# Retention two halves denser, outputs turned in the narrow chunk, and gates of the second half with silu at eviction

## What is computed

```
for l in range(DEPTH):                                  # 2 layers
    mod = silu(c) @ w_mod[l] + b_mod[l]                 # 2048 x 6144
    shift, scale, gate = split(mod, 3)
    h = rmsnorm(x, norm_gain[l]) * (1 + scale) + shift
    proj = h @ w_in[l]                                  # 2048 x 7504
    q_a, k_a, v_a, g_a, q_i, k_i, w_i, q_b, k_b, v_b, g_b = split(proj)
    y_a = sparse_attention(...) * silu(g_a)             # 8 heads of 128
    ret = retention(rotary(q_b), rotary(k_b) * SCALE, v_b)   # 8 heads of 128
    y_b = head_groupnorm(ret, ret_norm_gain[l]) * silu(g_b)
    x = x + gate * (concat(y_a, y_b) @ w_out[l])        # 2048 x 2048
```

## Time and profile before

| | us |
|---|---|
| median of 3 runs | 1963.54 |
| lowest, highest | 1959.96, 1964.26 |
| the profiled execution's own time | 1960.76 |
| span of its trace | 1959.0 |
| PE, DVE, ACT, POOL busy | 1877.9, 1363.6, 966.3, 326.2 |

### The profile page before, as it was taken

One profiled execution on the slowest core, in us unless ns is written; L12 is line 12 of the kernel. 1 busy time (PEld: TensorE's weight loads), 2 busy tenths in 40 slices (PEclk: granted clock), 3 DMA queues, 4 the chain that ended last, 5 costly groups with the idle time before them and its releaser, 6 DMA issues.

```text
span 1959.0 us, 24539 instructions
## 1 busy us (share of the span) xinstructions
PE 1877.9 (96%) x9056; PEld 1565.5 (80%) x9056; DVE 1363.6 (70%) x1953; ACT 966.3 (49%) x1307; POOL 326.2 (17%) x395
## 2 busy tenths in 40 slices
PE   4989999999888999999999999999999999999995
PEld 4878778888766877888878888888888888878884
DVE  8989989887788996755565544488775466564544
ACT  5454455444524444554454544566664445443643
POOL 0000002182203000217220000044440020030000
PEclk9999999999988999999999999999999999999998
DMA  9979967766585994654455555554445555556551
GB/s 351 355 247 345 348 226 275 280 221 212 197 309 184 340 356 163 195 168 155 144 178 188 189 193 193 194 172 151 150 152 179 193 184 180 189 182 213 184 174 65
DMA packets 210767, 420.08 MB, mean 214 GB/s; under 512 B 7136, under 2 KB 12012, under 8 KB 209772
## 3 DMA queue, kind: packets, MB, share of 16 engines
q1 hardware_dynamic: 209004, 413.08, 62.6%
q10 hardware_dynamic: 1664, 5.66, 0.8%
HBM read 416.59 MB, written 2.11 MB: 214 GB/s over the span
## 4 chain that ended last, share of the span: by engine, by line
PE 91%; DVE 6%; ACT 1%; issue 1%; POOL 0%; DMA 0%; DVEq 0%; ACTq 0%; POOLq 0%
PE acc L585 27%; PE acc L587 27%; PE acc L586 27%; DVE scr L1644 2%; PE tps L679 2%; DVE w_lo L1525 1%; PE sps L892 1%; PE sps L706 1%; PE tps L626 1%; PE tps L557 1%; PE acc L706 0%; PE tps L730 0%; PE sps L756 0%; DVE proj L1617 0%; PE sps L755 0%
## 5 line engine op out<-in xcount | busy, mean ns | idle before, releaser
L1525 DVE TENSOR_TENSOR w_lo<-raw,w_hi 128x1024 fp32r<-128x1024 f32 (+1 forms) x596 | 757.7, 1279 | 513.8 <-ACT w_hi L1069 501.4
L1069 ACT ACTIVATE w_hi<-raw 128x1024 fp32r<-128x1024 f32 (+1 forms) x596 | 623.5, 1051 | 801.4 <-PE acc L587 694.7
L585 PE MATMUL acc<-w_hi,ht_hi 128*128 128x512 f32 (+1 forms) x2384 | 946.4, 397 | 19.0 <-DVE proj L1888 9.0
L587 PE MATMUL acc<-w_hi,ht_lo 128*128 128x512 f32 (+1 forms) x2384 | 929.2, 390 | 0.0
L586 PE MATMUL acc<-w_lo,ht_hi 128*128 128x512 f32 (+1 forms) x2384 | 927.4, 389 | 0.0
L585 PEld LDWEIGHTS acc<-w_hi,ht_hi 128*128 128x128 f32 x2384 | 450.6, 189 | 109.8 <-issue 13.6
L587 PEld LDWEIGHTS acc<-w_hi,ht_lo 128*128 128x128 f32 x2384 | 449.7, 189 | 94.1
L586 PEld LDWEIGHTS acc<-w_lo,ht_hi 128*128 128x128 f32 x2384 | 450.9, 189 | 87.1
L1644 DVE SCALAR_TENSOR_TENSOR scr<-raw,vcol,scr 128x512 f32<-128x512 f32 x294 | 210.2, 756 | 7.5 <-DMA raw<-in_w_mod 0.2
L2237 POOL TENSOR_TENSOR scr<-scr 128x128 f32<-128x128 f32 x56 | 31.0, 585 | 157.6 <-DVE scr L1972 157.6
L2211 POOL TENSOR_TENSOR xres<-xres,proj 128x1024 f32<-128x1024 f32 x8 | 20.9, 2614 | 149.1 <-DVE proj L1888 149.1
(11 more groups left out here) (260 smaller groups left out, 1419.6 us busy)
## 6 DMA issues: line engine op xcount, KB each, us to landing
raw<-in_w_in SPq DMA_DIRECT2D x208, 1024.0 KB, 5.1
raw<-in_w_mod SPq DMA_DIRECT2D x96, 1024.0 KB, 6.8
raw<-in_w_out SPq DMA_DIRECT2D x32, 1024.0 KB, 5.1
raw<-in_w_o SPq DMA_DIRECT2D x16, 1024.0 KB, 5.1
raw<-in_w_ple_gate SPq DMA_DIRECT2D x16, 1024.0 KB, 5.0
raw<-in_w_b_out SPq DMA_DIRECT2D x8, 1024.0 KB, 5.0
raw<-in_w_a_out SPq DMA_DIRECT2D x8, 1024.0 KB, 5.0
raw<-in_w_in SPq DMA_DIRECT2D x8, 672.0 KB, 4.2
```

What stands on the lines that cost most here:

```text
L585: pe.matmul(o, hi_m, w_hi[:, slot, u, 0:width], start=start, stop=False)
L587: mm = pe.matmul(o, lo_m, w_hi[:, slot, u, 0:width], start=False, stop=stop)
L1069: act.activation(w_hi[:, x % SPL, :, 0:width], raw[:, j, 2 * (x % halves):2 * (x % halves) + 2, 0:width], ACT.Copy).then_inc(hi_ready, 1)
L1525: dve.tensor_tensor(w_lo[:, x % SPL, :, 0:width], raw[:, j, 2 * (x % halves):2 * (x % halves) + 2, 0:width], w_hi[:, x % SPL, :, 0:width]. ...
```

## The change

1. **Retention** starts a pair every 4 halves, not every 6. PE makes outputs of a pair together with the turning of the next one. The fourth pair ends in u = 22, half 6 of the narrow chunk.
2. **Outputs** are transposed on PE straight from `proj`, with no copy on POOL. Six of the eight pairs of tiles are turned after halves 1 to 6 of the narrow chunk (`early_side`), the last two after halves 3 and 4 of k = 15 (`late_side`). POOL multiplies the retention outputs by their gate in place, two heads at a time.
3. **Gates** of retention get silu in the eviction of k = 12, 13 and 14. The eviction of k = 12 is cut in two instructions, a copy and a silu.
4. **Evictions.** The narrow chunk's eviction on ACT is no longer at the end of its call, but in the iteration of half 3 of k = 15. `drain` is gone from `gemm`. Buffers of `acc` alternate through all calls.
5. **Pieces of modulation** in layer 0: two in k = 6 (none before), two in k = 12 (one before), one in k = 13 (three), three each in k = 15 (none), 16 and 17 (four each), two in k = 18 (four). A group that ends in k = 12 is summed by PE after half 2 of k = 12; the last group after half 3 of k = 18.

The core of the diff:

```diff
-PIECES = [{1: FULL, 2: FULL, 3: FULL, 4: FULL, 5: FULL, 8: (1, 3, 7), 9: (1, 3, 7), 10: (1, 3, 7), 11: (1, 3, 7),
-           12: (7,), 13: (1, 3, 5), 16: FULL, 17: FULL, 18: FULL}, {1: FULL, 2: FULL, 3: FULL, 4: FULL}]
+PIECES = [{1: FULL, 2: FULL, 3: FULL, 4: FULL, 5: FULL, 6: (1, 3), 8: (1, 3, 7), 9: (1, 3, 7), 10: (1, 3, 7),
+           11: (1, 3, 7), 12: (1, 3), 13: (7,), 15: (1, 5, 7), 16: (1, 3, 7), 17: (1, 3, 7), 18: (1, 3)},
+          {1: FULL, 2: FULL, 3: FULL, 4: FULL}]
...
                         if k == 11:
-                            SUM_AT[n], TAKE_AT[n] = (l, 12, 3), (l, 12, 7)
-                        if k == 13:
-                            SUM_AT[n], TAKE_AT[n] = (l, 14, 5), (l, 14, 7)
+                            SUM_AT[n], TAKE_AT[n] = (l, k, 1), (l, k, 5)
+                        if k == 12:
+                            SUM_AT[n], TAKE_AT[n] = (l, k, 2), (l, k, 6)
+                        if k == 18:
+                            SUM_AT[n], TAKE_AT[n] = (l, k, 3), (l, k, 7)
...
+                base = taken.n % 2
...
-                        buf = x // group % 2
+                        buf = (x // group + base) % 2
...
-                if drain:
-                    pe.wait_ge(acc_taken, taken.ahead(2))
...
-                p, n = u // 6, u % 6
-                if u == 0 or u == 6:
+                p, n = u // 4, u % 4
+                if 4 <= u <= 16 and n == 0:
...
+                if u < 16 and n == 0:
                     pe.wait_ge(mod_taken, m_taken.ahead(1))
...
+            def last_retention(l):
+                turned_early = early_side(0, output_columns, gated_outputs(l))
...
-                gemm(1, chunk_halves(1), 8, at=(l, 14), width=TAIL, side=lambda t, x, first: retention(l, 16 + x), drain=False)
+                gemm(1, chunk_halves(1), 8, at=(l, 14), width=TAIL, side=last_retention(l))
                 if l == 0:
-                    pe.wait_ge(mod_taken, m_taken.ahead(1))
-                    gemm(1, chunk_halves(2), 8, at=(l, 15), turning=0, drain=False)
+                    gemm(1, chunk_halves(2), 8, at=(l, 15), ready=early_ready,
+                         side=late_side(output_columns, gated_outputs(l)))
                     gemm(1, chunk_halves(2), 8, at=(l, 17))
...
+                def up12(g, b):
+                    cut = 0 if g else GB - 12 * CH
+                    if cut:
+                        act.activation(proj[:, :, 12 * CH:GB], acc[:, b, :, 0:cut], ACT.Copy)
+                    act.activation(proj[:, :, 12 * CH + g * CH + cut:12 * CH + (g + 1) * CH], acc[:, b, :, cut:CH],
+                                   ACT.Silu).then_inc(acc_taken, 1)
...
-                        act.activation(proj[:, :, GB:GB + DA], proj[:, :, GB:GB + DA], ACT.Silu).then_inc(ga_ready, 1)
...
-                turn(NH // 2, proj_tile(GA))
-                pool.wait_ge(yb_ready, ybr.next(8))
-                pool.wait_ge(ga_ready, 2 * (l + 1))
-                pool.wait_ge(acc_taken, accs.next(4))
-                turn(NH // 2, lambda o, k: pool.tensor_tensor(o, proj[:, :, ds(VB + k * P, P)], proj[:, :, ds(GB + k * P, P)],
-                                                              ALU.mult))
+                for p in range(NH // 2):
+                    if p == 0 or p == 2:
+                        pool.wait_ge(acc_taken, accs.next(1 if p else 3))
+                    pool.wait_ge(yb_ready, ybr.next(2))
+                    y, gb = (proj[:, :, a + p * S:a + (p + 1) * S] for a in (VB, GB))
+                    pool.tensor_tensor(y, y, gb, ALU.mult).then_inc(yg_ready, 1)
```

More of the change, by code:

```diff
@@ L543, in _, with gemm @@
             t_in, t_lo = Seen(pe, turn_in), Seen(pe, turn_lo)
-            def gemm(turns, halves, group, width=CH, side=None, side_per=None, at=None, drain=True,
-                     turning=None, turned_x=False, ready=None):
+            def gemm(turns, halves, group, width=CH, side=None, side_per=None, at=None, turning=None,
+                     turned_x=False, ready=None):
                 def turn_pair(p):
@@ L671, in _, with mod_sums @@
             m_ready = Seen(pe, mod_ready)
-            def mod_sums(src, b, parts=1):
+            def mod_sums(src, parts=1):
                 pe.wait_ge(mod_taken, m_taken.next())
@@ L719, in _ @@
                 pe.wait_ge(raw_read, lo.next(8))
-                mod_sums(macc, i % 2, parts=2)
+                mod_sums(macc[:, i % 2, :, :], parts=2)
                 if i == 2:
@@ L822, in retention @@
             def retention(l, u):
-                p, n = u // 6, u % 6
-                if u == 0 or u == 6:
+                p, n = u // 4, u % 4
+                if 4 <= u <= 16 and n == 0:
+                    for b in range(2):
+                        h = 2 * (p - 1) + b
+                        pe.wait_ge(rst_ready, rs.next())
+                        pe.wait_ge(acc_taken, 2 + (NCH + 1 + 4) * l + (12 if p <= 2 else 13))
+                        v = [proj[:, m, VB + h * HD:VB + (h + 1) * HD] for m in range(M)]
+                        pe.matmul(sps[:, b, 0:P], rst[:, b, 0:P], v[0], start=True, stop=True)
+                        pe.matmul(sps[:, b, P:S], rst[:, b, P:S], v[0], start=True, stop=False)
+                        pe.matmul(sps[:, b, P:S], rst[:, b, S:S + P], v[1], start=False,
+                                  stop=True).then_inc(ret_out, 1)
+                if u < 16 and n == 0:
                     pe.wait_ge(mod_taken, m_taken.ahead(1))
@@ L843, in retention, with gated_outputs, wait, output_columns @@
                                   stop=True).then_inc(rs_ready, 1)
-                    if n == 4:
-                        pe.wait_ge(rst_ready, rs.next())
-                        pe.wait_ge(acc_taken, 2 + (NCH + 1 + 4) * l + (12 if p < 2 else 13))
-                        v = [proj[:, m, VB + h * HD:VB + (h + 1) * HD] for m in range(M)]
-                        pe.matmul(sps[:, b, 0:P], rst[:, b, 0:P], v[0], start=True, stop=True)
-                        pe.matmul(sps[:, b, P:S], rst[:, b, P:S], v[0], start=True, stop=False)
-                        pe.matmul(sps[:, b, P:S], rst[:, b, S:S + P], v[1], start=False,
-                                  stop=True).then_inc(ret_out, 1)
+            def gated_outputs(l):
+                def wait(p):
+                    if p == 0:
+                        pe.wait_ge(y_ready, yr.ahead(2))
+                    if p >= NH // 2:
+                        pe.wait_ge(yg_ready, NH // 2 * (l - 1) + p + 1)
+                return wait
+            def output_columns(k, m):
+                col = GA + k * HD if k < NH else VB + (k - NH) * HD
+                return proj[:, m, col:col + HD]
+            def last_retention(l):
+                turned_early = early_side(0, output_columns, gated_outputs(l))
+                def side(t, x, first):
+                    retention(l, 16 + x)
+                    turned_early(t, x, first)
+                return side
             for l in range(DEPTH):
@@ L1016, in last_side @@
                     early_pair(0, embedding_columns, embedded)
-            gemm(1, chunk_halves(2), 8, side=last_side, drain=False)
+            gemm(1, chunk_halves(2), 8, side=last_side)
             pe.wait_ge(turn_lo, t_lo.ahead(2))
@@ L1038, in _ @@
             results = Seen(act, split_used, SPL)
+            groups = [0]
             t_out = Seen(act, turned, 2)
@@ L1054, in split @@
                 gb = nh // group
+                base = groups[0] % 2
+                groups[0] += turns * gb
                 def take(g, b):
@@ L1295, in retention @@
                 def retention(u):
-                    if u % 6 == 4 and u < 24:
+                    if u % 4 == 0 and 8 <= u <= 20:
+                        for b in range(2):
+                            act.wait_ge(ret_out, rout.next())
+                            if NH * l + u // 2 > 4:
+                                act.wait_ge(yb_ready, NH * l + u // 2 - 4)
+                            for m in range(M):
+                                q = C_QG + m * NH + 2 * (u // 4 - 2) + b
+                                r = act.activation(ro[:, b, m, :], sps[:, b, m * P:(m + 1) * P], ACT.Copy,
+                                                   scale=kst[:, q:q + 1])
+                            r.then_inc(ret_taken, 1)
+                    if u % 4 == 0 and 4 <= u < 20:
                         for b in range(2):
```

184 lines of the change are left out of this document (93 added, 91 removed).

## The result

The changed kernel takes 1948.91 us, the median of 4 runs (1945.02 to 1950.10), against 1962.4 us for the kernel before in the same measurement (1959.96 to 1964.26). The ratio is 0.9929, with a 95% interval of 0.9910 to 0.9947. It is faster by 13.5 us. The forecast was 1945.3, 18.2 us less than before, in a range of 1940.0 to 1956.5. In a later measurement the same kernel took 1948.26 against 1960.64: 12.4 us less, ratio 0.9937 [0.9923, 0.9951].

The account below looks back on a forecast made before the run. PE, busy for 96% of the span, bounds the kernel. Removing 25.0 us of waits, less 0.95, 5.6 and 0.3, saves 18.2: from the median 1963.5 to 1945.3 us, range 1940 to 1956.5.

Parts of the forecast that it names:

- end of the narrow chunk, layer 0: End of narrow chunk into k = 15: 6.0 us of PE waits, behind ACT's eviction, table load and silu, would go.
- k = 17: Layer 0: PE's wait for DVE's eviction, 9.1 us, and 1.6 of lower clock behind it would go, 10.7 together.
- k = 12: Layer 0: new PE waits on DVE, 1.6 us ahead of half 2 and 4.0 at the sum, +5.6 together.
- k = 6 and 7: Two pieces in k = 6 take DVE 5.2 us; no cost to PE forecast, 1 kept for the range.
- so the wait goes, and not only the `drain`: k = 15 to 18, layer 0: fewer pieces give DVE reserve, so PE's wait goes, not just the instruction waiting for eviction.
- 2.4 more if the clock falls: k = 12, layer 0: possible extra 2.4 us from a low clock behind the wait, not in the 5.6 taken.
- first rival: Longer wait in k = 12 (7.1 + 2.4 us) and 2 in the narrow chunks: 1951 us, chance 0.14.
- just enough: k = 15, layer 0: DVE's work of 22.9 us would fit within PE's 23.6.
- if DVE has no gaps in k = 15 to 18: Layer 0: one of the signs that would show the prediction wrong.
- near 3: Chunks behind k = 15, layer 0: DVE's reserve in us, with three pieces taking 19.9 against PE's 22.7.
- rival on loads: Narrow chunk: a table switch costs a second 1.28 outside its row, some 2 us a layer; 1949 us, chance 0.04.
- slower case: Pairs four halves apart: PE waits for masks at each of eight outputs, 38 us; 1983 us, chance 0.05.

Follow-up runs that it names:

- changed: Stage column from the first profile of the changed kernel, against the kernel before; the profiled execution took 1945.02 us.
- again: Stage column from a second profile of the unaltered changed kernel, in the later measurement; 1948.26 us, ratio 0.9937 to the kernel before.
- experiment 1: Kernel before without drain ahead of k = 17: 1953.86 us; changed kernel with that wait put back: 1957.42; with pieces laid out nearly as before: 1949.30.

## Why the prediction was right, and where it was off

The time fell into the range, and every gain came where it was forecast and at its size, within 0.6 us; the forecast is 3.6 us too low, and the saving 4.7 to 5.8 us too large. Measured terms are worked out from the stages of "changed" and "again":

| term (us) | forecast | measured |
|---|---|---|
| end of the narrow chunk, layer 0 | -6.0 | -6.6 |
| the same, layer 1 | -6.0 | -6.4 |
| k = 17 | -10.7 | -10.6 |
| wait in k = 13 | -2.3 | -2.3 |
| last sum | +0.95 | +0.95 |
| k = 12 | +5.6 | +8.0, +9.2 |
| narrow chunk tight | +0.3 | 0 |
| behind half 5 of k = 15 | 0 | +1.6 |
| k = 6 and 7 | 0 | +0.4, +0.8 |
| between the layers | 0 | +1.4 |

With -0.1 to -0.3 in layer 1, k = 0 to 11, these add up to -13.9 and -12.1; the medians say -13.5 and -12.4.

*The gains.* The earlier trace rows gave both narrow chunks, the 10.7, the 2.3. One sentence about them was wrong: "so the wait goes, and not only the `drain`" made DVE's missing reserve half of the cause. DVE had indeed no reserve, and even less than the 22.8 against 22.7 us of the budget, which left out some 2.2 that POOL's addition costs it in such a chunk (4.56 for 2.35). But that is worth 1.4 to 1.6 us a chunk (experiment 1); the rest is the drain. With a piece less the wait for that eviction shrinks from 9.0 to 6.3 us and doesn't go.

*The step that failed most* is "2.4 more if the clock falls": it stood as a bound and should have stood in the sum. Both waits came out at their size, 1.40 and 4.40, since the durations under POOL were the right ones to take and the run without rotary shows why. But every stop of this kind that was seen in layer 0's k = 12 was followed by a low clock: of seven profiles with the two waits (6.0 us together), two lost 2 us more to it, five 3 to 4. With it the term is 8 to 10, which takes in the 9.5 that the first rival had for k = 12, and with the 2.4 of the prediction the forecast would have been about 1948. That rival's 7.1 is itself added wrongly: two pieces of 4.51 for 4.00 make 5.6 into 6.6.

*Half 5 of k = 15.* The budget of DVE, 22.9 against 23.6, ended "just enough" because it was made at the price "With POOL idle". POOL's products by the gates make three `w_lo` take 5.58 and not 3.5 us. With these 2.1 the budget is 25.0, against 23.6, and DVE was busy for 24.95 of 25.30 us: the sign of being wrong "if DVE has no gaps in k = 15 to 18" all but came true in this chunk. In k = 16 to 18 POOL's addition costs as much, so that three pieces come to 22.1 and not 19.9 us against PE's 22.7, and the "near 3" of reserve was 0.6; in k = 17 DVE is busy for 21.99 of 22.58 us. The wait shows where a piece and the end of a group, 3.5 us, stand straight ahead of the low parts that PE needs next, and 0.7 of it goes without the table load ahead of the eviction. DMA, at 0.97, is as full as DVE there. No run took POOL's product out of k = 15; the 2.1 are read from the rows.

*The missed term* is the table load between the layers. I counted the eight additional loads (the traces have 56 for 48, not 44 for 36), priced those ahead of the first tiles and looked for the others nowhere. The rival on loads had its place wrong: in the narrow chunk the loads cost nothing. One costs 1.0 us between the layers, and its cause, the silu, lies nearly 100 us earlier; the one ahead of that silu costs 0.7 in k = 15. Of the 2.66 us that "ScalarE: Activation LUTs" of the Trainium skill (What ACT_TABLE_LOAD costs) gives for a switch the trace again shows the load alone: 1.28 us, and 1.0 us of path between the layers. The page also advises to batch work by table set (Table sets: the hidden batching unit); the change does the opposite, and these two places are what it pays for it.

*k = 6.* Two pieces are 5.7 us at the price of an idle POOL (2 x 2.87), not 5.2; PE lost 0.4 to 0.8 us in k = 7, inside the 1 kept for it.

*The slower case* was wrong in layer 1 and in layer 0 behind k = 12: pairs four halves apart never wait for masks there.

## What to carry to other kernels

After an edit that changes which function an engine ran last, follow that state to its next use, however far: a hidden load can turn up on a path where nothing else runs. Price a stop of several microseconds on TensorE with the slow clock behind it in the sum, not as a bound. Where small work may stand anywhere, put it behind the step that another engine waits for (here the masks), and keep it out of chunks in which both VectorE and DMA are full: with the table load made early, that gave as much again as the whole change. A budget of VectorE needs the long instructions that GpSimd runs beside it: one of 3.3 us cost it some 2.2 us here.
